# A two-layer diffusion step on one core: the state-space stage as one stream of 24 units, eight adaLN slots moved into the expert preamble, zeros read from HBM padding

## What is computed

```python
def ada_mod(cond, w, b):
    return (jax.nn.silu(cond) @ w + b)[:, None, :]

def trunk_layer(x, mod, g_mix, g_ffn, mixer, p, moe_p, pos, ctx):
    sh1, sc1, gt1, sh2, sc2, gt2 = jnp.split(mod, 6, axis=-1)
    h = rms_norm(x, g_mix) * (1 + sc1) + sh1
    out, state = mixer(h, p, pos, ctx)
    x = x + gt1 * out
    h = rms_norm(x, g_ffn) * (1 + sc2) + sh2
    return x + gt2 * moe_ffn(h, *moe_p), state

# in ssd_scan, per chunk of 128 tokens and per direction (16 heads):
decay = jnp.exp(jnp.where(mask, seg, -jnp.inf))
scores = jnp.einsum('bcihn,bcjhn->bcijh', ch, bh) * decay
y_diag = jnp.einsum('bcijh,bcjhp->bcihp', scores, xdt)
states = jnp.einsum('bcjhn,bcjh,bcjhp->bchpn', bh, decay_end, xdt)
y_off = jnp.einsum('bcihn,bchpn,bcih->bcihp', ch, s_in, jnp.exp(cum))
# in ssd_mixer:
y = y_f + rev(y_b) + x * d_skip
y = rms_norm(y * jax.nn.silu(z), p['ssd_norm'])
```

## Time and profile before

| | |
|---|---|
| median of 3 runs | 1118.93 us (1117.82 to 1126.79) |
| the profiled execution | 1129.93 us, of which the span is 1128.1 us |
| TensorE | 934.3 us busy, 83% of the span |
| VectorE | 372.4 us, 33% |
| ScalarE | 289.5 us, 26% |
| moved by DMA | 259 MB, mean 230 GB/s |
| TensorE's mean granted clock | 0.911 of full speed |

### The profile page before, as it was taken

How to read it: one execution, slowest core, us unless ns; L and a number is a source line. 1 busy time by engine, 2 the same in 40 slices (tenths; PEclk the granted TensorE clock), 3 DMA queues, 4 the chain that set the end, 5 groups by cost and what they waited for, 6 DMA issues and landing times.

```text
span 1128.1 us, 14055 instructions
## 1 busy us (share of the span) xinstructions
PE 934.3 (83%) x5625; PEld 497.8 (44%) x5625; DVE 372.4 (33%) x924; ACT 289.5 (26%) x684; POOL 50.2 (4%) x63
## 2 busy tenths in 40 slices
PE   5999984968879789963989996897998963999994
PEld 1455642746635455532323325454545532333324
DVE  0422003747547650051111112364663151111112
ACT  1421021232425550041101111222663141101110
POOL 0400000000000000102000002000000102000002
PEclk8999996978879899985999997898799985999997
DMA  9999996442447401317599987106000316599925
GB/s 385 427 425 413 410 418 288 167 170 97 183 189 273 175 1 56 112 57 278 230 415 424 424 346 292 54 1 233 0 1 1 112 57 276 224 421 425 421 119 187
DMA packets 36339, 258.99 MB, mean 230 GB/s; under 512 B 3408, under 2 KB 3552, under 8 KB 21424
## 3 DMA queue, kind: packets, MB, share of 16 engines
q1 hardware_dynamic: 20448, 198.27, 43.8%
q0 software_dynamic: 12224, 47.01, 10.5%
q10 hardware_dynamic: 3600, 12.78, 2.8%
HBM read 203.17 MB, written 54.87 MB: 229 GB/s over the span
## 4 chain that ended last, share of the span: by engine, by line
PE 68%; DVE 12%; DMA 8%; ACT 6%; issue 3%; another core or an unknown queue 1%; POOL 1%; SPq 0%; DVEq 0%; POOLq 0%; ACTq 0%
PE ps L474 20%; PE ps L586 13%; PE ps L608 8%; PE ps L828 6%; DMA U<-expert_rows 3%; PE ps L488 3%; PE ps L661 2%; PE ps L570 2%; DMA ring<-w_in 2%; PE ps L513 2%; PE ps L747 2%; PE ps L438 2%; PE ps L495 1%; DVE U L1538 1%; ACT U L936 1%
## 5 line engine op out<-in xcount | busy, mean ns | idle before, releaser
L586 PE MATMUL ps<-ring,U 128*32 128x512 f32 x1200 | 166.3, 592 | 0.0
L474 PE MATMUL ps<-U,ring 128*128 128x384 f32 x320 | 105.1, 487 | 2.7 <-DVE U L1317 1.4
L608 PE MATMUL ps<-ring,U 128*32 128x512 f32 x672 | 85.7, 594 | 0.0
L586 PEld LDWEIGHTS ps<-ring,U 128*32 128x32 f32 x1200 | 47.5, 110 | 85.3 <-issue 84.7
L474 PEld LDWEIGHTS ps<-U,ring 128*128 128x128 f32 x320 | 60.0, 189 | 47.4 <-issue 4.2
L586 PE MATMUL ps<-hT,U 128*32 128x512 f32 x168 | 73.1, 592 | 0.0
L586 PE MATMUL ps<-U 128*32 128x512 f32 x168 | 73.1, 592 | 0.0
L828 PE MATMUL ps<-ring,hT 128*128 128x384 f32 x192 | 66.0, 504 | 5.7 <-ACT hT L906 4.9
L474 PE MATMUL ps<-hT,ring 128*128 128x384 f32 x208 | 68.6, 488 | 1.0 <-issue 1.0
L570 PE MATMUL ps<-small,U 128*128 128x128 f32 x192 | 30.8, 312 | 45.4 <-DMA U<-expert_rows 43.4
L438 PE MATMUL ps<-ring,cond_w 128*32 128x384 f32 x512 | 55.8, 559 | 14.1 <-ACT cond_w L883 8.7
(11 more groups left out here) (250 smaller groups left out, 1323.0 us busy)
## 6 DMA issues: line engine op xcount, KB each, us to landing
ring<-w_in SPq DMA_DIRECT2D x102, 1536.0 KB, 11.4
expert_rows<-U POOLq DMA_DIRECT2D x16, 2048.0 KB, 77.6
U<-expert_rows SPq DMA_DIRECT2D x24, 512.0 KB, 6.9
expert_rows<-U ACTq DMA_DIRECT2D x24, 512.0 KB, 9.5
hT<-w_in SPq DMA_DIRECT2D x6, 1536.0 KB, 12.3
U<-w_in SPq DMA_DIRECT2D x6, 1536.0 KB, 15.9
small<-small_in SPq DMA_DIRECT2D x1, 3147.5 KB, 34.2
xT<-x_in SPq DMA_DIRECT2D x1, 1536.0 KB, 16.7
```

The costliest lines, as they stand in the source:

```text
L474: ins = mm(out, lhs(k), rhs(k), start=(k == 0), stop=(k == n - 1))
L586: ins = mm(ps[q:q + 32, r, :], xgT[:, r, P * k + q:P * k + q + 32], w[e][:, c:c + 512], start=(k == 0), stop=(k == DC - 1))
L608: ins = mm(ps[q:q + 32, 6 + h, :], actT_of[i % NR][:, P * j + q:P * j + q + 32], w[e][:, c:c + 512], start=(j == 0), stop=(j == 1))
```

## The change

1. **One stream.** The 24 units of the three full tiles are numbered through (U = 0 to 23). The end of tile i is done among the first units of tile i + 1: the sum with banks 5 and 6 ahead of its first scores, the product with z and the sum of squares at unit 0, the normalisation at unit 2, the transposes at unit 4. The states' part (`off`) is added one piece a unit, at units 2 to 5 of the tile's own (`OFF_AT`), the state updates stand at fixed units (`STATE_AT`), the next tile's transposes at unit 5 and its correlations at unit 7. `ytok`, `xw` and `ytmp` get places of their own (in `oTy` and in columns of `xc` that are no longer read).
2. **adaLN.** The 14 slots of the stage stand at units 0, 1, 3, 4, 5, 7, 9, 11, 13, 15, 17, 18, 20 and 22. The 8 slots of the MLA preparation move into layer 0's expert preamble: two behind the sum of squares, one behind the router, one behind the transposes for the scatter, four behind the positions. In the ring they now come behind the output projection's four slots, just ahead of the experts'.
3. **Zeros.** The clearing DMAs read from the unused last 1024 columns of an existing slot in HBM; the memset goes, and so does VectorE's wait.
4. **Opening.** GpSimd adds the squares (`sum_chunks(0, 0)`), the sum of squares stands ahead of adaLN slot 4, `dk` moves behind chunk 5 of the projection, and the large load of `small` goes behind the first projection slot.

```diff
-        xw = ytok = oTm[:, 0:1024]
-        ytmp = oTm[:, 1024:1536]
+        ytok = [oTy3[:, :, P * t:P * t + P] for t in range(NT)]
+        ytmp = [xc3[:, 4 * g:4 * g + 4, 129:257] for g in range(2)]
+        xw = {(0, 1): ytok[1], (1, 0): ytok[2], (3, 0): xc3[:, 0:8, 129:257], (3, 1): xc3[:, 0:8, 257:385]}
...
+        N_UNIT = 24
+        OFF_AT = {2: (0, 0), 3: (0, 1), 4: (1, 0), 5: (1, 1)}
+        STATE_AT = {(1, 6): 0, (3, 3): 0, (3, 4): 1}
...
-        for _i in (1, 2, 3):
-            POINTS += [(("unit", _i, _u), 1) for _u in ((-1, 2, 5) if _i == 1 else (-1,))] + [(("tail", _i), 2), (("end", _i), 1)]
-        POINTS += [(("mla", _k), 1) for _k in range(N_PREP + 1)]
+        POINTS += [(("unit", _u), 1) for _u in (0, 1, 3, 4, 5, 7, 9, 11, 13, 15, 17, 18, 20, 22)]
+        POINTS += [(("moe", 0), 2), (("moe", 1), 1), (("moe", 2), 1), (("moe", 3), 4)]
...
             def row_of_slot(n):
+                if S_OUTE - N_MOE_ADA <= n < S_OUTE - N_MOE_ADA + N_OUTE:
+                    return n + N_MOE_ADA
+                if S_OUTE - N_MOE_ADA + N_OUTE <= n < S_MOE0:
+                    return n - N_OUTE
...
-                if n == N_FIRST - 1:
+                if n == N_FIRST:
                     sp.dma_start(small[:, N_SMALL_FIRST:], small_d[:, N_SMALL_FIRST:]).then_inc(S["in_small"], 16)
...
             for n in range(N_FIRST):
-                if n == N_FIRST - 1:
+                if n == N_SQUARE + 1:
                     sum_squares(0, 0)
                 ada(n)
...
+            turn_in(0)
+            late_ada("state")
+            cums(0)
+            cums(1)
+            state(0, 1)
+            turn_in(1)
+            correlate(1)
+            for U in range(N_UNIT):
+                i, u = U // 8 + 1, U % 8
+                if U + 2 < N_UNIT:
+                    cums(U + 2)
+                diag(U)
+                if OFF_AT.get(u) and STEPS[i][0]:
+                    from_state(i, *OFF_AT[u])
+                if (i, u) in STATE_AT:
+                    state(i, STATE_AT[i, u])
+                late_ada("unit", U)
+                if i > 1 and u == 4:
+                    turn_out(i - 1)
+                if i < 3 and u == 5:
+                    turn_in(i + 1)
+                if i < 3 and u == 7:
+                    correlate(i + 1)
+            turn_out(3)
...
-            dve.wait_ge(S["row_cleared"], 16 * (NE * CAP // 512))
...
+            dve.wait_ge(S["xtok_ready"], 1)
+            weigh(0, 1)
+            dve.sem_inc(S["xtok_used"], 1)
+            segment(0)
+            segment(1)
+            update(0, 1)
+            for U in range(N_UNIT):
+                i, u = U // 8 + 1, U % 8
+                if u == 0:
+                    if i > 1:
+                        add_diagonal(i - 1)
+                    dve.wait_ge(S["xtok_ready"], i + 1)
                     for d in range(2):
+                        link(tt(cut(xdt[d], HS), cut(xtok, HS), spread(e96[2][:, col(i, d)], PS), MUL))
+                scores(U)
+                if U + 2 < N_UNIT:
+                    segment(U + 2)
+                if i > 1 and u == 0:
+                    gate_with_z(i - 1)
...
             def clear_rows():
-                zero = oTm[:, 0:D]
-                pool.memset(zero, 0.0).then_inc(S["cleared"], 1)
-                pool.wait_ge(S["cleared"], 1)
+                zero = w_d[S_OUTO + 2, :, 2 * D:SLOT]
                 pool.wait_ge(S["h_scaled"], DC)
```

More of the change, by code:

```diff
@@ L43 @@
 N_FIRST = 6
+N_MOE_ADA = 8
+N_SQUARE = 3
+DK_AFTER = 5
 S_INE = S_ADA0 + N_FIRST
@@ new lines, in diag @@
+            def diag(U):
+                u, q, d = U % 8, U % 8 // 2, U % 2
+                pe.wait_ge(S["s_ready"], U + 1)
+                for h in range(4):
+                    hh = 4 * (q % 2) + h
+                    ins = mm(ps[:, 5 + q // 2, 64 * hh:64 * hh + 64], dec[U % 3][:, P * h:P * h + P],
+                             xdt[d][:, 64 * (4 * q + h):64 * (4 * q + h) + 64],
+                             start=(u % 4 == 0 and h == 0), stop=(d == 1), skip_group_check=True)
+                ins.then_inc(S["diag_done"], 1)
@@ L1083, in _, with turned_in @@
             late_rows("cum")
-            nfull = 0
             ssdn = sm("ssd_norm")
-            for i, (t, full) in enumerate(STEPS):
+            def turned_in(i):
                 if i:
@@ new lines, in _ @@
+            turned_in(0)
+            late_rows("state")
+            decay(0)
+            decay(1)
+            turned_in(1)
+            correlated(1)
+            for U in range(N_UNIT):
+                i, u = U // 8 + 1, U % 8
+                if U + 2 < N_UNIT:
+                    decay(U + 2)
+                if i > 1 and u == 0:
+                    square_sum(i - 1)
+                late_rows("unit", U)
+                if i > 1 and u == 4:
+                    turned_out(i - 1)
+                if i < 3 and u == 5:
+                    turned_in(i + 1)
+                if i < 3 and u == 7:
+                    correlated(i + 1)
```

453 lines of the change are left out of this document (243 added, 210 removed).

## The result

The changed kernel takes 1139.9 us (median of 4 runs, 1138.44 to 1141.55) beside 1122.86 us for the kernel before (4 runs, 1117.82 to 1129.56): ratio 1.0143, 95% interval 1.0095 to 1.0191. The forecast was 1091 and a gain. The profiled execution lies at 1139.8 us, span 1138.2, mean granted clock 0.886 (before 0.911).

What follows compares the result with a forecast made beforehand. TensorE, busy 83% of the span, was taken as the bound, so only its waits could yield time. Terms -4.3 - 12.5 - 3.6 - 14.8 + 0 + 7.5 = -27.7 us gave 1102.2 profiled, median 1091; range 1080 to 1110.

Steps and rivals of the forecast that it cites:

- Opening, -4.3: Kernel start: squares taken earlier let weight slot 5's matmuls start at 30.2 us, winning 4.3 us (3 to 5).
- Clearing wait and head, -12.5 and -3.6: State-space stage start: VectorE's wait for zeros goes, 12.5 us; less work before the first scores wins 3.6.
- Units, -14.8: First scores to MLA preparation: TensorE sets the pace at full clock, 115 us instead of 129.5, winning 14.8.
- The stream adds instead of overlapping: Rival for the units: slot time is added, not hidden; stream 127 us, sum -15.5, total 1103 us; 20%.
- I am wrong if the unit stream takes over 125 us: Sign set beforehand: a unit stream over 125 us would show the forecast wrong.
- MLA preparation, 0: Eight adaLN slots leave the preparation: 2.6 us to gain, up to 4 lost at low clock; taken as 0.
- Expert preamble, +7.5: Layer 0's expert preamble: four late slot loads ahead of the rows delay the first expert matmul 7.5 us (3 to 11).
- The ring's delay paid in full: Rival for the expert stage: eight slots less in the ring cost 30 us, not 7.5; total 1114; 10%.
- the clearing starves the weights: Rival: HBM-to-HBM clearing copies slow weight loads; at four times the hold, 37 us lost, total 1128; 5%.
- The base: Sums made against the profiled execution, 1129.93 us; its 11 us over the median 1118.93 taken off the median forecast too.

Runs made afterwards that it cites:

- experiment 1: Kernel before with only the new opening and the zeros copied from HBM padding, old stage order and slots; 1113.98 us, ratio 0.9927.
- g3: Experiment 2 plus unused matmuls: seven before the first unit, two ahead of the diagonal product after units without a slot; 1108.15 us, ratio 0.989.
- h1: g3 plus nine unused matmuls before the last tile's transposes, in the bank these take next; 1110.33 us, ratio 0.9896.
- k3: Changed kernel with rows loaded ahead of expert slots 4 to 7 and unused matmuls filling the stream's waits; 1107.65 us, ratio 0.9875.
- experiment 2: Changed kernel with the eight adaLN slots back in the MLA preparation and the old ring order; 1122.9 us, ratio 0.9984.
- experiment 3: Changed kernel with SyncE waiting for the scatter and loading the rows ahead of expert slots 4 to 7; 1122.99 us, ratio 0.999.
- experiment 4: Changed kernel, each expert-preamble adaLN slot's eight matmuls replaced by one small one, loads and order unchanged; 1140.45 us, ratio 1.0192.
- g4: Experiment 1 plus eight unused matmuls in bank 7 at each of the three tile ends; 1125.22 us, ratio 1.0049.
- experiment 10: Experiment 2 with each unit's adaLN slot moved ahead of its diagonal product, no work added; 1117.75 us, ratio 0.9965.
- e4: Changed kernel with the TensorE work of the stage's 14 adaLN slots left out but for one small matmul each, weights still loaded; single execution, 1124.82 us.
- e1: Same run as experiment 1: kernel before with only the new opening and zeros from HBM; 1113.98 us, ratio 0.9927.
- e2: Same run as experiment 2: changed kernel with the eight adaLN slots back in the MLA preparation; 1122.9 us, ratio 0.9984.
- e3: Same run as experiment 3: changed kernel with the rows loaded ahead of expert slots 4 to 7; 1122.99 us, ratio 0.999.
- h5: Same run as experiment 4: changed kernel without the large matmuls of the preamble's eight adaLN slots; 1140.45 us, ratio 1.0192.

## Why the prediction was wrong

*Opening, -4.3:* slot 5's matmuls start at 30.16, as forecast (30.2), and the second group of matmuls behind the normalisation moved from 46.62 to 42.40, 4.2 us. It depends on the clock as well: experiment 1, with the same code, won 1.5, because its sums and slot 4 ran at half clock (1.63, 1.49 and 2.46 us instead of 0.89, 0.81 and 1.50).

*Clearing wait and head, -12.5 and -3.6:* right within about a microsecond; the first weighting starts at 174.41, the head takes 10.2 us instead of the 9.4 forecast, scores forecast near 184 come at 184.60. The 2 MB copies from HBM to HBM landed 88.5 us after their issue in the median instead of 77.6, the last of them 157.0 instead of 136.9, and the stretch from 100 to 160 us moved 376 GB/s against 411. So the zeros are there at about 206 us instead of 190.8. They reach the first units but starve nothing: TensorE waits for no weight slot in the stage. The Trainium skill's figure (DMA: Bandwidth & Descriptors, Latency and other measured facts), by which I estimated that the clearing would end some 80 us later, does not hold here: it ended 15 us later.

*Units, -14.8: this is the step that failed.* "I add up each engine's work on it at full clock" took 101 us of TensorE work and 14 of waits. Measured: 123.3 busy at a mean clock of 0.75, which is an estimated 92 us of work at full clock (busy time by mean clock), and 22 of waits. So the low clock cost some 31 us and the waits 8 more than forecast, and 9 came back because the work had been put too high: together about the 30.6 us by which this step missed. What the sum lacked was the clock. I had priced the low clock in the MLA preparation, where it did not matter, and not in the stage, although gave 0.85 for it. That the clock is a cause is shown by g3, h1 and k3: more work, shorter stage. By the medians the filling gives back 10 to 15 us (g3 against experiment 2, k3 against experiment 3), by single profiles 11 to 20. The rest of the miss, 10 to 12 us against the forecast's 115, was not recovered; it holds the filling's own work and waits, and is not taken apart. Part of the waits may be of the same origin, since a slow slot puts off the cums that VectorE waits for.

*The stream adds instead of overlapping (127 us):* its mechanism is not what is seen, since VectorE's work at the tile ends now lies beside TensorE's (85% and 55% busy in the same stretch). Its time, 127, is near what h1 and k3 took with the clock kept up (125.1 and 126.7), by luck and not by its mechanism. No rival had the clock in it; "I am wrong if the unit stream takes over 125 us" was the right alarm.

*MLA preparation, 0:* right. 85.8 us to the output projection against 85.9.

*Expert preamble, +7.5:* the mechanism (four slots' loads ahead of the rows) was right, its size was 15.5. The term that was mis-sized is the bandwidth sum, which shared 421 GB/s out as if all came at the same time. The rows must wait for the scatter, and the scatter beside the slot loads took 21.1 us instead of 4.4 to its last landing; only then came the rows' own 3.7 us. Experiment 3 takes that away and is left with 3.9, at the low end of 3 to 11, although its last four slots ran at half clock, which the forecast had named for the 11; experiment 4 shows that with the loads as they were the slots' large matmuls are only 1.8 of the 15.5. The Trainium skill (DMA: Bandwidth & Descriptors, Queues, rings and completion order) says that each DMA engine takes turns between the queues' rows packet by packet; the 21.1 us beside 4.4 agree with that, though no run separates it from plain fullness.

*The ring's delay paid in full, the clearing starves the weights:* neither. The part behind the preamble took 589.8 us against 591.7.

*The base.* I took the 11 us between the profiled execution of before and its median as constant. The changed kernel's profile lay on its median; from profile to profile the change costs 9.9 us, from median to median 17. Two slips in the sums change nothing: 101 + 6 + 8 is 14.5 less than 129.5, not 14.8, and 3.7 (1 + 4) is 18.5, not 18.7.

With the two causes out of the way the kernel runs at 1107.65. The forecast of 1091 also held a stage of 115 us, 12 less than k3's, and that offset of 11 us.

## What to carry to other kernels

A sum of TensorE work at full clock leaves the clock out and is no forecast: where the work is small matmuls with waits of a microsecond between them, price it at the clock that the windows of the old profile show, and for a new order with more and smaller waits, at both levels. Where a wait can't be removed, unused work in it can pay (g3), and it can lose where its bank is not free at once (g4 waited 6.05 us for it). Work that must be done anyway would be better there than unused work, but experiment 10, which moved it so, is not clear of noise. Read one profile of a stage with caution: the same code took 135 to 145 us here. A scatter that something waits for should have no bulk loads issued beside it: with 6.3 MB of loads beside it its last landing went from 4.4 us to 21.1.

## What the runs showed of the hardware

- A short wait can be followed by a fall of the clock that costs more than the wait, but is not always. In g3 the clock fell after waits of 1.51 us (that ended at 224.39) and of 0.83 (247.05). In k3 the wait of 0.83 us that ended at 244.48 was followed by 15 us at 1.00. What decides it stays open.
- Small matmuls at 1.2 GHz can hold TensorE 99% busy without getting the clock back (e4, 220 to 230 us at 0.51), while in the changed kernel the clock was back at 1.00 from 210 us, behind an adaLN slot. Over the stage the clock was lower without the slots (0.59) than with them (0.75 to 0.82).
- Two pieces of the states' part on different row halves, side by side, took about half as long for each as the single one with 1.12 us: in e1 two took 1.13 us and the next two 1.02.
- Copies from HBM to HBM beside weight loads: sixteen pieces of 2 MB landed 84.6 to 91.4 us after their issue (medians) in all sixteen kernels that had them, the last one 149.0 to 158.4; from SBUF it was 77.6 and 136.9.
- Six indirect scatters, 3.1 MB in all, landed at most 4.4 to 4.5 us after their issue without bulk loads beside them (before, e1, e2, e3), and up to 21.1 and 17.5 with them (after, h5).
